# An FP32 encoder trunk on one core: the SBUF tiles of a running kernel laid out at other addresses

## The reference, cut to what matters

```python
def reference(x, ...):
    for i in range(2):
        hn = rmsnorm(x, mix_pre_g[i])
        y = pool_mixer(hn, ...) if i == 0 else mlstm_mixer(hn, ...)
        x = x + rmsnorm(y, mix_post_g[i])
        hn = rmsnorm(x, ffn_pre_g[i])
        y = sq_relu_mlp(hn, mlp_w1[i], mlp_w2[i])     # relu(hn @ w1)**2 @ w2
        x = x + rmsnorm(y, ffn_post_g[i])
    return x
```

## Time and profile before

| | us |
|---|---|
| median of 2 runs | 1915.82 (1913.63 to 1918.01) |
| the profiled execution | 1916.18 |
| its span, first to last instruction | 1914.4 |

### The profile page before, as it was taken

How to read it: one execution, slowest core, us unless ns; L and a number is a source line. 1 busy time by engine, 2 the same in 40 slices (tenths; PEclk the granted TensorE clock), 3 DMA queues, 4 the chain that set the end, 5 groups by cost and what they waited for, 6 DMA issues and landing times.

```text
span 1914.4 us, 24458 instructions
## 1 busy us (share of the span) xinstructions
PE 1883.8 (98%) x8526; PEld 1535.6 (80%) x8526; DVE 1343.7 (70%) x2120; ACT 1067.9 (56%) x1825; POOL 89.8 (5%) x121
## 2 busy tenths in 40 slices
PE   8999999999999999999999999999999999999999
PEld 6678888888888888888878888777888888888886
DVE  5877565655678987786866867777665656577875
ACT  7646555564445547766766757645555555445533
POOL 0110000000000200010000110020000000000010
PEclk9999999999999999999999999999999999999999
DMA  5344343448633533352323442245243436853353
GB/s 214 116 140 184 121 158 144 155 174 324 226 94 99 179 130 102 109 171 94 100 88 100 128 157 91 77 150 195 84 170 133 167 136 239 299 178 98 111 192 127
DMA packets 79706, 285.00 MB, mean 149 GB/s; under 512 B 9408, under 2 KB 9536, under 8 KB 71136
## 3 DMA queue, kind: packets, MB, share of 16 engines
q1 hardware_dynamic: 64288, 239.96, 35.8%
q0 software_dynamic: 8320, 27.27, 4.3%
q10 hardware_dynamic: 6976, 16.21, 2.8%
HBM read 211.51 MB, written 71.89 MB: 148 GB/s over the span
## 4 chain that ended last, share of the span: by engine, by line
PE 87%; DVE 8%; issue 2%; ACT 2%; DMA 0%; SPq 0%; DVEq 0%; ACTq 0%
PE bank L803 6%; PE bank L805 5%; PE bank L804 5%; PE core L1020 5%; PE core L1022 5%; PE core L1021 5%; PE core L971 5%; PE core L970 5%; PE core L972 5%; PE bank L1020 4%; PE bank L1022 4%; PE bank L1021 4%; PE bank L971 4%; PE bank L970 4%; PE bank L972 4%; PE bank L903 2%
## 5 line engine op out<-in xcount | busy, mean ns | idle before, releaser
L1467 ACT CAST h_hi<-h_raw 128x512 fp32r<-128x512 f32 x188 | 116.5, 620 | 236.0 <-PE core L1022 142.7
L1831 DVE TENSOR_TENSOR w_lo<-raw,w_hi 128x1024 fp32r<-128x1024 f32 x132 | 161.3, 1222 | 121.4 <-ACT w_hi L1281 119.2
L803 PE MATMUL bank<-x_hi,w_hi 128*128 128x512 f32 x560 | 226.1, 404 | 3.3 <-issue 2.8
L1281 ACT CAST w_hi<-raw 128x1024 fp32r<-128x1024 f32 x132 | 138.0, 1045 | 151.7 <-PE bank L805 46.5
L805 PE MATMUL bank<-x_hi,w_lo 128*128 128x512 f32 x560 | 219.8, 393 | 0.0
L804 PE MATMUL bank<-x_lo,w_hi 128*128 128x512 f32 x560 | 218.6, 390 | 0.0
L2088 DVE TENSOR_TENSOR h_lo<-h_raw,h_hi 128x512 fp32r<-128x512 f32 x188 | 129.7, 690 | 113.2 <-ACT h_hi L1467 113.2
L1020 PE MATMUL core<-h_hi,w_hi 128*128 128x512 f32 x464 | 181.8, 392 | 1.3 <-DVE y L2154 1.2
L1022 PE MATMUL core<-h_hi,w_lo 128*128 128x512 f32 x464 | 181.9, 392 | 0.0
L1021 PE MATMUL core<-h_lo,w_hi 128*128 128x512 f32 x464 | 181.4, 391 | 0.0
L1982 DVE TENSOR_TENSOR w_lo<-sums,w_hi 128x512 fp32r<-128x512 f32 x104 | 71.7, 689 | 97.8 <-ACT w_hi L1309 95.0
(11 more groups left out here) (334 smaller groups left out, 4386.3 us busy)
## 6 DMA issues: line engine op xcount, KB each, us to landing
raw<-weights SPq DMA_DIRECT2D x132, 512.0 KB, 3.3
h_pair_dram<-y SPq DMA_DIRECT2D x26, 1792.0 KB, 6.7
h_raw<-h_pair_dram SPq DMA_DIRECT2D x182, 256.0 KB, 2.8
w<-second_pairs SPq DMA_DIRECT2D x24, 768.0 KB, 4.4
raw_odd<-first_pairs SPq DMA_DIRECT2D x14, 1024.0 KB, 7.2
x_scratch<-y POOLq DMA_DIRECT2D x48, 256.0 KB, 2.5
raw<-first_pairs SPq DMA_DIRECT2D x12, 1024.0 KB, 7.1
xold<-x_scratch POOLq DMA_DIRECT2D x40, 256.0 KB, 3.6
```

The lines of the kernel that those rows point to most:

```text
L803: nc.tensor.matmul(o, a, hi(t), start=(k == 0), stop=False)
L1281: nc.scalar.copy(w_hi[:, ROW[u] * T:(ROW[u] + 2) * T], raw[:, (n % RAW) * BLK:(n % RAW + 1) * BLK]).then_inc(hi_ready, 1)
L1831: dve.tensor_tensor(w_lo[:, s], raw[:, (n % RAW) * BLK:(n % RAW + 1) * BLK], w_hi[:, s].bitcast(F32), ALU.subtract).then_inc(lo_ready, 1)
```

## The change

No instruction is added, removed or moved: each engine issues the same instructions in the same order with the same waits. The addresses change, and two operands of small things:

- the mask in `consts` is stored once for 128 tokens, not four times, and `rows_for` reads it four times with a step of zero; `consts` shrinks from 2560 to 1024 bytes, and its load with it
- `pool_bs`, `ssq` and `rs` move to right behind `consts`, and a tile `to_2048` of 64 bytes that nothing uses fills up to a multiple of 2048
- `ones` (512 bytes) moves behind all arenas.

```diff
-CONSTS = P + T
+CONSTS = 2 * P
...
-        mask = consts[:, C_MASK:C_MASK + T]
+        mask = consts[:, C_MASK:C_MASK + P].rearrange("p (o n) -> p o n", o=1).to_broadcast([P, CPH, P])
+        pool_bs = sb("pool_bs", [P, KT])
+        ssq = sb("ssq", [P, 2, HALVES * CPH])
+        rs = sb("rs", [P, HALVES * CPH])
+        sb("to_2048", [P, 16])
...
-        ones = sb("ones", [P, P])
-        pool_bs = sb("pool_bs", [P, KT])
-        ssq = sb("ssq", [P, 2, HALVES * CPH])
-        rs = sb("rs", [P, HALVES * CPH])
...
+        with ExitStack() as behind:
+            behind.enter_context(nc.sbuf_tensor("all_arenas", [P, 4 * PAIRS * T + (2 * H_RING + 6 + H_RAW) * T], F32))
+            ones = behind.enter_context(nc.sbuf_tensor("ones", [P, P], F32))
...
-                dve.tensor_tensor(mx_b[:, j % 2, :], mask, mx_b[:, j % 2, :], ALU.subtract).then_inc(mm_ready, 1)
+                by_chunk = mx_b[:, j % 2, :].rearrange("p (c n) -> p c n", c=CPH)
+                dve.tensor_tensor(by_chunk, mask, by_chunk, ALU.subtract).then_inc(mm_ready, 1)
...
-    constants = np.concatenate([np.eye(P, dtype=np.float32), *[causal] * CPH], axis=1)
+    constants = np.concatenate([np.eye(P, dtype=np.float32), causal], axis=1)
```

## The result

The changed kernel takes 1934.5 us (median of 2 runs, 1932.8 to 1936.2) against 1915.8 us: a ratio of 1.0098 with a 95% interval of 1.0067 to 1.013. It is slower by 1%, where I forecast 0.9% faster. Its profiled span is 1934.4 us for 1914.4.

What follows compares the result with a forecast made beforehand. TensorE's distance between fp32r matmul starts was taken as the bound. Savings of 16.9 us and 0.5 us, other terms 0, gave 1916.2 - 17.4 = 1898.8, so 1899 us against the median; range 1820 to 1952 us, about 0.8.

Steps and rivals of the forecast that it cites:

- What bounds the kernel: Whole kernel: TensorE, busy 1883.8 of 1914.4 us; time is 7584 fp32r matmuls times 229 ns between starts, 1736.7 us.
- The address of a tile can change that distance: fp32r matmuls: the moving tile's place alone can cost 4.5 ns per matmul, 1.9%.
- `early_h`: Only fp32r moving tile at 1344, 233.5 ns against 229.0; moving it to 0 saves 6.75 ns on 72 matmuls, 0.5 us.
- I take places as equal when they differ by 512 ... 64 bytes further give 2.25 ns: Moving tiles from 1984 to 0: line through two places gives 226.75 ns, saving 16.9 us over 7512 matmuls.
- Mask, small tiles, DMAs at 0: Step-zero mask read, `consts` load, moved small tiles and DMAs to shifted tiles: each forecast to cost 0 us.
- Nothing given back: TensorE's waits: gaps of 30.6 us in all have nearly nothing to give; the sum of 17.4 us counted in full.
- like `early_h`: Rival, all fp32r matmuls: the new place is another bad one, 233.5 ns, 33.8 us more, 1950 us; chance 0.16.
- The moving stream and the weight load meet: Rival: both reads starting close together, 128 bytes apart, may be worse; at 238 ns, 67.6 us more, 1984 us; chance 0.13.
- The whole excess goes: Rival: moving tiles no longer cross a multiple of 2048, so 215.7 ns, 101.2 us less, 1820 us with waits; chance 0.20 → stated 0.18.
- the class with 0.67: Whole-kernel time within 2% either way, between 1877.5 and 1954 us; chance 0.67.

Runs made afterwards that it cites:

- the map: Kernel of its own, x only copied: stretches of 48 back-to-back fp32r matmuls with moving and stationary tiles at chosen places; 226.7 to 233.3 ns between starts at multiples of 64 bytes.
- experiment 2: The changed kernel without its 64 bytes of padding, moving tiles at 1984 again, rest of the change kept: 1916.2 us, ratio 1.0013 to before.
- the one with D = 0: Changed kernel with 128 bytes more padding, so moving minus stationary address (D) is 0 modulo 256: 1900.8 us, ratio 0.9930 to before.

## Why the prediction was wrong

- **What bounds the kernel**: right. The time followed the distance between starts in every version; the chain, the clock and the other engines stayed.
- **The address of a tile can change that distance**: right. `early_h` was a true sign, and the page of the Trainium skill that speaks against it ("SBUF — State Buffer", "Who interferes with whom": two independent read ports, PE waits on no one) does not describe fp32r matmuls as they ran here.
- **"I take places as equal when they differ by 512 ... 64 bytes further give 2.25 ns"**: this is the step that failed. From two points I drew a line for the moving tile's own place. I had taken the stationary tile's place as without effect, since pieces 512 bytes apart ran alike; but 512 is two periods of 256, so those rows could not show an effect. What counts is the difference between the two places, and the function repeats every 256 bytes and goes up and down. In the map the moving tile at 0 has 232.4 and its neighbour at 128 has 226.7 with the same weights. The term was forecast at -16.9 us and was about +26 us.
- **`early_h`**: forecast at -0.5 us, it went from 396 to 395 ns; too small to tell in the total.
- **Mask, small tiles, DMAs at 0**: right within the 0.13% of experiment 2; in its profiled execution the second rhythm accounts for the difference in TensorE's busy time. The plain FP32 matmuls at the end stayed at 428 to 430 ns per record.
- **Nothing given back**: partly wrong. 5.7 of 25.7 us came out of gaps. With them, 20.0 us remain.
- **The rivals**: "like `early_h`" (0.16) named a new bad place and 1950 us; it was the closest, with 3.5 ns for 4.5 and no allowance for gaps. "The moving stream and the weight load meet" (0.13) had the right variable, the difference of the two places, but its reason, nearness, is refuted (64 apart costs 233.3, 0 apart costs 226.7) and its 1984 us too. "The whole excess goes" is refuted for every place tried: the least excess over 215.7 is 10.9 ns.
- The time lay in the range and in the class with 0.67, but on the wrong side of no change.

What stays open: why the two addresses interact with a period of 256 bytes in fp32r while bf16 shows nothing at the places tried, where the 11 ns that are left at D = 0 come from, and what decides between two rhythms. A stream of fp32r matmuls without any weight load between them wasn't tried.

## What to carry to other kernels

With fp32r operands and back-to-back matmuls of 128x512 (at 256 columns another D was best), put the moving tiles and the stationary pieces at the same address modulo 256; here it is worth 0.7% over one placing and 1.7% to 2.0% over two others, for a few bytes of padding. Alignment to a round number by itself is worth nothing: the changed kernel aligned one operand to 2048 and lost 1%. When a trace shows two rates for one instruction, hold one operand and move the other before drawing a line through them, and change a small tile ahead of large ones only with a look at what it shifts.

## What was new about the hardware

- The distance between fp32r matmuls of 512 columns went from 226.6 to 240.0 ns with the places of the operands alone, at full granted clock and with nothing else running. Steps of 4 bytes matter (226.7 at D = 0, 238.1 at D = 4).
- At one D the stream can run in two steady rhythms, 228.9 and 233.3 ns at D = 64. A kernel at such a place may take one or the other from stage to stage, and change over without a pause. The ten runs of the kernel without padding spread over 9.6 us, the five of the one with D = 0 over 4.2; that the rhythms are the reason is not shown.
- Narrowing the stationary operand from 128 to 16 columns did not shorten the distance at D = 0 (226.7 to 228.9 ns) and took 1.6 ns off at D = 192 (233.3 to 231.7).
